# The choice matrix of a further turn moved onto the output buffer, in a one-core encoder layer with 32 experts

## The chip, the cores and the metric

The kernel runs on one core of a Trainium2 chip. The core has five engines, each with an instruction stream of its own: TensorE (matmuls), VectorE, ScalarE, GpSimd and SyncE. They meet through semaphores; 16 DMA engines move data between HBM and SBUF, fed by queues that SyncE (called SP in the profile), ScalarE (ACT) and GpSimd (POOL) issue into. In the profile TensorE is PE, its weight loads are PEld, VectorE is DVE. The metric is the device time of one execution in microseconds, the median of several.

## What is computed

One layer of an encoder, on two requests of 256 tokens each (512 tokens, 1024 values per token, f32): a modulated norm, a projection with spatial gating and pooling, a norm, and then a mixture of 32 experts of which every token takes two. The part that matters here is the last one:

```python
def _hier_moe(h, ...):                       # h: 512 x 1024
    g_sel = argmax(h @ w_router_group)       # one of 4 groups
    top_logit, top_idx = top_k(logits of the 8 experts in the group, 2)
    gate = p_sel * softmax(top_logit)
    ...
    for each expert e, for its tokens xs:
        ys = (silu(xs @ w_exp_gate[e]) * (xs @ w_exp_up[e])) @ w_exp_down[e]
    out[token] += ys * weight
y = LN(alpha * x + gate2 * out)
```

The weights of an expert are two matrices of 1024 x 512 and one of 512 x 1024, f32, 2 MB each.

## The kernel before

The first 450 us or so are the norm, the projection and the mixer; the change doesn't touch them. Behind them runs a loop over the 32 experts, written out in the program of each engine.

**A turn.** An expert works on up to 64 tokens (`CAP`) at a time. TensorE gathers their rows by a matmul with a matrix of zeros and ones (the choice matrix) that VectorE makes by comparing slot numbers, `gate_up` multiplies by `gate_w` and `up_w` (side by side in the two halves of the array), ScalarE takes the silu into `sg_hid`, VectorE multiplies the two halves (`sg_hid<-bank,sg_hid`, L2033), TensorE transposes the product (line 926), ScalarE copies it to `hid_t`, TensorE multiplies by `down_w`, and VectorE evicts the result into `yout`, times a gate that it has written there before (lines 1963, 1965 and 2048). GpSimd stores `yout` to `round_y` in HBM. At the end the rows are gathered from `round_y` and summed.

**Which experts.** Every expert has this main turn. One with more than 64 tokens has further turns, on the same weights with other buffers, all of them with an x in their names: `sel_x` (the choice matrix, 2 KB per partition), `x_rows_x`, `x_t_x` and `hid_t_x` (gathered rows, their transpose, the hidden values) and `yout_x` (the output, 2 KB per partition). In SBUF `x_rows_x`, `x_t_x`, `hid_t_x` and `sel_x` begin at the same place, T0; `yout_x` lies at T0 + 4096. The table `tab` holds for each expert the number of its further turns (`tab[0:1, 0, e]`) and the number of those of all earlier experts (`tab[0:1, 1, e]`). With these inputs there is exactly one further turn in the whole run, that of expert 19; VectorE writes `yout_x` in it (line 2010) once.

**Branches.** For experts 2 to 31 each engine loads the number of further turns and goes either through the plain path or, by a jump to code at the end of its program, through `with_further`, where the main turn and the first further one are interleaved. There TensorE begins with `further_selected`, the gathering matmuls that read `sel_x`.

**What VectorE does for the next expert.** Since a jump is made late, VectorE writes the choice matrix of a possible further turn for every expert from 2 on, whether it has one or not: `further_ahead` (line 1974), ahead of the branch and ahead of the product `sg_hid` of that expert. In the trace this is `sel_x<-next_slots,slot_of`, line 1976, 30 times.

**Waits.** VectorE does its instructions in order, so one that waits holds all behind it. The semaphores of the further turns are `x_sem[...]`: "yo" counts the finished `yout_x` (it starts at 1), "xs" the finished gathering matmuls. `x_st` counts the stores of `yout_x`: it stands at 16 after a small store early in the kernel, and a further turn adds 32, for two stores of 128 KB (lines 570 and 571). Before the change VectorE waits for `x_st` in `further_gate`, before it writes the gate into `yout_x`. TensorE in plain experts does `gate_up`, then a part of the gathering for later experts (`sel_group`), then the transposes of `sg_hid`, the rest of that gathering and the matmuls with `down_w`.

**Weights.** SyncE loads `gate_w` and `up_w` three experts ahead into three buffers, each when the `gate_up` that read the buffer is done (lines 413 and 414), and `down_w` two ahead into two buffers, when the matmuls that read it are done (line 417).

Of the kernel before, what the change touches and what calls it, by code (L numbers as in the profile page):

```python
# [11 lines left out]
TILES = TOK // 128  # L12
# [7 lines left out]
CAP = 64  # L20
ASSIGN = 2 * TOK
FURTHER = ASSIGN // CAP
# [18 lines left out]
def hybrid_encoder(nc, x_prompt, x_sample, c_prompt, c_sample, w_mod, b_mod, w_in, b_in, w_spatial,  # L41
# [3 lines left out]
    bf16, f32, f32r, i32, u32 = mybir.dt.bfloat16, mybir.dt.float32, mybir.dt.float32r, mybir.dt.int32, mybir.dt.uint32  # L45
# [8 lines left out]
    with ctx:  # L54
        base = (nc.sbuf_base + 63) // 64 * 64

        def at(name, shape, dt, off):
            return nc.alloc_sbuf_tensor_at(name, shape, dt, offset=base + off)

        def sem(name):  # L60
            return ctx.enter_context(nc.semaphore(name))
# [69 lines left out]
        tab = at("tab", [1, 2, NEXP + 1], i32, S0 + 2528)  # L131
        slots = at("slots", [128, CAP], f32, S0 + 2816)
        next_slots = at("next_slots", [128, CAP], f32, S0 + 2048)
        T0 = S0 + 9728
# [49 lines left out]
        slot_of = at("slot_of", [128, NEXP, TILES], f32, S0 + 1536)  # L184
        hid_t_x = at("hid_t_x", [128, FC, CAP], f32, T0)
        sg_hid = at("sg_hid", [128, DE], f32, T0 + 36864)
        sel_x = at("sel_x", [128, TILES, 2, CAP], f32r, T0)
        yout = [at(f"yout{i}", [128, 512], f32, o) for i, o in enumerate((T0 + 2048, S0 + 3584, S0 + 5632))]
        x_rows_x = at("x_rows_x", [128, 512], f32, T0)
        x_t_x = at("x_t_x", [128, 2, 4, CAP], f32, T0)  # L190
# [105 lines left out]
        x_st = sem("x_st")  # L296
# [3 lines left out]
        x_sem = {n: sem("x_" + n) for n in ("sl", "xs", "xr", "xtr", "xt", "gum", "silu", "hid", "htr", "ht", "ym", "yo")}  # L300
# [1233 lines left out]
        def _(dve):  # L1534
# [368 lines left out]
            def chosen_pair(out, columns):  # L1903
                return dve.tensor_tensor(out[:, :, :, :],
                                         slots[:, :].rearrange("p (i a s) -> p i a s", i=1, a=1).broadcast_to([128, TILES, 2, CAP]),
                                         columns.rearrange("p a (i s) -> p i a s", s=1).broadcast_to([128, TILES, 2, CAP]), ALU.is_equal)
# [54 lines left out]
            def gate_of_slots(out, first_sem, count, of_first, of_second):  # L1961
                dve.wait_ge(first_sem, count)
                dve.tensor_scalar(out[:, :], gate2_half[1][:, :], of_second, None, ALU.mult).then_inc(first_sem, 1)
                dve.wait_ge(first_sem, count + 1)
                dve.scalar_tensor_tensor(out=out[:, :], in0=gate2_half[0][:, :], scalar=of_first, in1=out[:, :],
                                         op0=ALU.mult, op1=ALU.add).then_inc(first_sem, 1)
                dve.wait_ge(first_sem, count + 2)
# [4 lines left out]
                return more, first  # L1972

            def further_ahead(e):
                dve.wait_ge(dve_selx, 1)
                dve.tensor_tensor(sel_x[:, :, :, :],
                                  next_slots[:, :].rearrange("p (i a s) -> p i a s", i=1, a=1).broadcast_to([128, TILES, 2, CAP]),
                                  slot_of[:, e, :].rearrange("p (i a s) -> p i a s", a=1, s=1).broadcast_to([128, TILES, 2, CAP]),
                                  ALU.is_equal).then_inc(dve_selx, 1)

            def further_counted(e):
                column = slot_of[:, e, :]
                dve.tensor_scalar(column, column, float(CAP), None, ALU.subtract).then_inc(dve_gx, 1)
                dve.tensor_scalar(n0[:, e:e + 1], n0[:, e:e + 1], float(CAP), None, ALU.subtract).then_inc(dve_gx, 1)

            def further_chosen(e, turns):
                further_counted(e)
                column = slot_of[:, e, :]
                dve.wait_ge(x_sem["yo"], turns + 1)
                dve.wait_ge(dve_gx, 6 * turns + 2)  # L1990
                chosen_pair(sel_x, column.rearrange("p (a i) -> p a i", a=1).broadcast_to([128, 2, TILES])).then_inc(x_sem["sl"], 1)

# [4 lines left out]
            def further_gate(e, turns):  # L1997
                dve.tensor_scalar(side[:, 0, 3:4], n0[:, e:e + 1], -0.5, None, ALU.is_gt).then_inc(dve_gx, 1)
                dve.tensor_scalar(side[:, 1, 3:4], n0[:, e:e + 1], -0.5, None, ALU.is_le).then_inc(dve_gx, 1)
                dve.wait_ge(x_sem["yo"], turns + 1)  # L2000
                dve.wait_ge(x_st, 32 * turns + 16)
                gate_of_slots(yout_x, dve_gx, 6 * turns + 4, side[:, 0, 3:4], side[:, 1, 3:4])

            def further_hidden(turns):
# [7 lines left out]
            def further_round(e, turns):  # L2012
                further_chosen(e, turns)
                further_columns(turns)
                further_gate(e, turns)
                further_hidden(turns)
                further_out(turns)
# [32 lines left out]
            def with_further(e):  # L2050
                more, first = turns_of(e)
                dve.wait_ge(dve_g, 2 * (e // 3 + 1) + 2 * e)
                dve.wait_ge(dve_selx, e)
                further_counted(e)
                dve.wait_ge(dve_gx, 6 * first + 2)
                dve.sem_inc(x_sem["sl"], 1)
                further_columns(first)
                hidden(e)
                gate_rows(e)
                further_gate(e, first)  # L2060
                further_hidden(first)
                out_rows(e)
                next_group(e)
                further_out(first)
                with dve.If(more > 1):
                    with dve.Fori(1, more) as r:
                        further_round(e, dve.snap(first + r))

            def expert(e):
# [14 lines left out]
                elif e == 1:  # L2084
                    dve.tensor_scalar(next_slots[:, :], slots[:, :], float(CAP), None, ALU.add).then_inc(dve_selx, 1)
                    hidden(e)
                    dve.wait_ge(m_sem["yo"], e)
                    gate_rows(e)
                    for half, bank in enumerate((B[2], B[4])):
                        dve.wait_ge(m_sem["xtr"], 4 + half)  # L2090
                        columns_in(x_by_expert[:, 2:4, 4 * half:4 * half + 4, :], bank).then_inc(m_sem["xt"], 1)
                    chosen_group(4)
                    out_rows(e)
                else:
                    more = dve.value_load(tab[0:1, 0, bass.ds(e, 1)], min_val=0, max_val=7)
                    dve.wait_ge(m_sem["yo"], e)
                    if e % 3 == 0:
                        sides(e)
                    further_ahead(e)
                    parted(dve, f"dve_{e}", more)  # L2100
                    hidden(e)
                    gate_rows(e)
                    out_rows(e)
                    next_group(e)
                    joined_again(dve, f"dve_{e}")
# [146 lines left out]
```

## Time and profile before

| | us |
|---|---|
| median of 3 runs | 959.89 |
| lowest, highest | 959.08, 962.08 |
| the profiled execution | 962.08 |
| its span, first to last instruction | 960.4 |

The profiled execution is the run with the highest time. TensorE is busy 908.7 us of the span (95%), VectorE 376.8, ScalarE 244.7, GpSimd 113.7. The profile lists groups of instructions with the idle time of their engine just before them and the engine that ended it; "issue" there is a wait that nothing recorded explains. The chain of waits follows the work that ended last back to the start. The granted clock is TensorE's, as a share of 2.4 GHz; it has two levels, 1 and 0.5 (1.2 GHz). The time from a DMA's issue to its landing is listed by tile. Experts are counted from 0 in this text; the 32 evictions of `yout` on VectorE tell in the trace where each ends: expert 18's starts at 733.35 us, expert 19's at 764.26, expert 20's at 782.44.

### The profile page before, as it was taken

The numbers are of one execution on the slowest core, as the hardware profiler recorded it, in microseconds if no ns is written. First come the engines' busy times: TensorE is split into PE (matmuls) and PEld (weight loads), VectorE is DVE, ScalarE is ACT, GpSimd is POOL, SyncE is SP. The second block draws the span as 40 slices with busy tenths as digits, with TensorE's granted clock in tenths as the row PEclk, the third lists the DMA queues.
The fourth block names the chain that finished last, engine by engine and source line by source line (L and its number), as shares of the span: only waits on it lengthen the run. The fifth ranks groups of instructions, "written<-read, shape, count | busy, mean of one in ns | idle before, by whom it ended". The sixth has DMA issues, their size and how long they took to land.

```text
span 960.4 us, 11747 instructions
## 1 busy us (share of the span) xinstructions
PE 908.7 (95%) x4381; PEld 548.4 (57%) x4381; DVE 376.8 (39%) x646; ACT 244.7 (25%) x357; POOL 113.7 (12%) x142
## 2 busy tenths in 40 slices
PE   3999999999999999999999999998997999998994
PEld 2567776888888888786444444444444343443331
DVE  4533443565344236798532232222221221322235
ACT  1432244432233225446411111101101110111024
POOL 2210366000001000000000000000100000000031
PEclk9999999999999999999999999999997999999997
DMA  9985655265565623809999999999999799999974
GB/s 370 347 276 175 257 215 177 90 231 206 202 237 149 180 93 115 274 0 411 388 397 400 419 426 428 426 425 428 427 428 424 307 420 425 426 427 427 422 295 138
DMA packets 47510, 295.53 MB, mean 308 GB/s; under 512 B 5046, under 2 KB 7190, under 8 KB 32082
## 3 DMA queue, kind: packets, MB, share of 16 engines
q1 hardware_dynamic: 37216, 263.99, 68.3%
q0 software_dynamic: 9616, 29.02, 9.0%
q10 hardware_dynamic: 610, 1.66, 0.5%
q8 instruction: 38, 0.62, 0.3%
q14 instruction: 30, 0.25, 0.1%
HBM read 275.81 MB, written 23.09 MB: 311 GB/s over the span
## 4 chain that ended last, share of the span: by engine, by line
PE 89%; DVE 4%; issue 3%; DMA 2%; ACT 2%; POOL 0%; ACTq 0%; POOLq 0%; DVEq 0%
PE bank L624 85%; PE bank L926 2%; DMA cst<-in_consts 1%; DMA y_first<-round_y,pos_y 1%; PE bank L654 1%; DVE st L1558 0%; PE bank L829 0%; PE bank L689 0%; DVE wo_lo L1752 0%; DMA round_y<-yout,store_row 0%; PE bank L908 0%; DVE y_second L2166 0%; DVE y_second L2179 0%; ACT w_hi L1170 0%; POOL y_second L612 0%
## 5 line engine op out<-in xcount | busy, mean ns | idle before, releaser
L624 PE MATMUL bank<-down_w,hid_t 128*64 128x512 f32 x512 | 122.0, 619 | 12.5 <-issue 9.8
L624 PE MATMUL bank<-h_hi,w_hi 128*128 128x512 f32 x320 | 124.8, 390 | 0.3 <-ACT h_hi L1204 0.3
L624 PE MATMUL bank<-h_hi,w_lo 128*128 128x512 f32 x320 | 124.7, 390 | 0.0
L624 PE MATMUL bank<-h_lo,w_hi 128*128 128x512 f32 x320 | 124.5, 397 | 0.0
L624 PE MATMUL bank<-gate_w,x_by_pair 128*64 128x512 f32 x256 | 112.5, 592 | 0.8 <-ACT x_by_pair L1170 0.8
L624 PE MATMUL bank<-up_w,x_by_expert 128*64 128x512 f32 x256 | 112.6, 593 | 0.0
L624 PE MATMUL bank<-gate_w,x_by_expert 128*64 128x512 f32 x256 | 112.6, 593 | 0.0
L624 PE MATMUL bank<-up_w,x_by_pair 128*64 128x512 f32 x256 | 112.5, 592 | 0.0
L1587 DVE TENSOR_TENSOR w_lo<-raw,w_hi 128x1024 fp32r<-128x1024 f32 x56 | 68.5, 1225 | 76.6 <-ACT w_hi L1170 76.5
L1404 ACT ACTIVATE sg_hid<-bank 64x512 f32<-64x512 f32 x33 | 19.5, 592 | 310.2 <-PE bank L624 310.2
L2033 DVE TENSOR_TENSOR sg_hid<-bank,sg_hid 64x512 f32<-64x512 f32 x32 | 22.2, 695 | 176.9 <-ACT sg_hid L1404 176.8
L596 POOL DMA_INDIRECT round_y<-yout,store_row x31 | 31.9, 1028 | 494.8 <-DVE yout L2048 469.4
L624 PEld LDWEIGHTS bank<-down_w,hid_t 128*64 128x64 f32 x512 | 36.9, 141 | 73.5 <-issue 67.4
L624 PEld LDWEIGHTS bank<-gate_w,x_by_pair 128*64 128x64 f32 x256 | 35.0, 137 | 71.2 <-issue 71.2
L624 PEld LDWEIGHTS bank<-gate_w,x_by_expert 128*64 128x64 f32 x256 | 34.8, 137 | 70.3 <-issue 70.1
L2048 DVE TENSOR_TENSOR yout<-bank,yout 128x512 f32<-128x512 f32 x32 | 22.1, 691 | 132.7 <-PE bank L624 128.1
L624 PEld LDWEIGHTS bank<-h_lo,w_hi 128*128 128x128 f32 x320 | 60.1, 188 | 24.3 <-issue 11.7
L1170 ACT ACTIVATE w_hi<-raw 128x1024 fp32r<-128x1024 f32 x56 | 58.9, 1053 | 52.6 <-PE bank L624 51.6
L624 PEld LDWEIGHTS bank<-h_hi,w_lo 128*128 128x128 f32 x320 | 60.1, 188 | 12.8
L624 PEld LDWEIGHTS bank<-h_hi,w_hi 128*128 128x128 f32 x320 | 60.1, 188 | 12.5 <-ACT h_hi L1204 0.7
L624 PE MATMUL bank<-sel_group,h_hi 128*128 128x256 f32 x224 | 61.2, 307 | 0.0
L624 PEld LDWEIGHTS bank<-sel_group,h_hi 128*128 128x128 f32 x224 | 42.4, 189 | 23.6 <-issue 21.9
(329 smaller groups left out, 1313.6 us busy)
## 6 DMA issues: line engine op xcount, KB each, us to landing
down_w<-in_w_exp_down SPq DMA_DIRECT2D x32, 2048.0 KB, 18.0
gate_w<-in_w_exp_gate SPq DMA_DIRECT2D x30, 2048.0 KB, 18.0
up_w<-in_w_exp_up SPq DMA_DIRECT2D x30, 2048.0 KB, 22.7
modraw<-in_w_mod SPq DMA_DIRECT2D x24, 1024.0 KB, 7.1
raw<-in_w_in SPq DMA_DIRECT2D x9, 2048.0 KB, 9.7
round_y<-zrow POOLq DMA_DIRECT2D x6, 2048.0 KB, 7.7
raw<-in_w_branch_b SPq DMA_DIRECT2D x2, 2048.0 KB, 9.4
raw<-in_w_branch_a SPq DMA_DIRECT2D x2, 2048.0 KB, 10.6
```

Of the source, the lines that this page charges most:

```text
L596: pool.indirect_dma_start(round_halves, bass.IndirectOffsetOnAxis(store_row[:, e:e + 1], 0), yout[s][:, :], None, bounds_check=2 * LAST_RO ...
L624: return pe.matmul(out, lhsT, rhs, start=start, stop=stop, skip_group_check=True)
L654: x = pe.transpose(bank[:, 128 * (kc % 4):128 * (kc % 4) + 128], xin[:, i, 128 * kc:128 * kc + 128], ident)
L926: x = pe.transpose(bank[:, CAP * fc:CAP * fc + CAP], view[:, fc, :], ident[CAP:128, CAP:128])
L1170: return act.activation(out, in_, ACT.Copy, scale=scale)
L1404: act.activation(sgb[0:CAP, :], bank[0:CAP, :], ACT.Silu).then_inc(sm["silu"], 1)
L1587: dve.tensor_tensor(w_lo[par][:, :, :], raw[:, u % 2, :, 128 * (b % 4):128 * (b % 4) + 128], w_hi[par][:, :, :].bitcast(f32), ALU.subtract ...
L2033: dve.tensor_tensor(sg_hid[CAP:128, :], B[0][CAP:128, :], sg_hid[0:CAP, :], ALU.mult).then_inc(m_sem["hid"], 1)
L2048: dve.tensor_tensor(yout[s][:, :], B[1][:, :], yout[s][:, :], ALU.mult).then_inc(m_sem["yo"], 1)
```

## The change

`sel_x` moves from T0 to T0 + 4096, where `yout_x` lies. It no longer overlaps `x_rows_x`, `x_t_x` and `hid_t_x`. VectorE then may write `sel_x` only when the `yout_x` of the last further turn has been stored, so `further_ahead` loads the number of earlier further turns and waits for `x_sem["yo"]` and `x_st`; `further_chosen`, which is used for second and later turns, waits for `x_st` too; and `further_gate`, which writes `yout_x`, waits until the gathering matmuls have read `sel_x` instead of waiting for the store.

```diff
-        sel_x = at("sel_x", [128, TILES, 2, CAP], f32r, T0)
+        sel_x = at("sel_x", [128, TILES, 2, CAP], f32r, T0 + 4096)
...
             def further_ahead(e):
+
+                first = dve.value_load(tab[0:1, 1, bass.ds(e, 1)], min_val=0, max_val=FURTHER)
+                dve.wait_ge(x_sem["yo"], first + 1)
+                dve.wait_ge(x_st, 32 * first + 16)
                 dve.wait_ge(dve_selx, 1)
                 dve.tensor_tensor(sel_x[:, :, :, :],
...
                 dve.wait_ge(x_sem["yo"], turns + 1)
+                dve.wait_ge(x_st, 32 * turns + 16)
                 dve.wait_ge(dve_gx, 6 * turns + 2)
...
             def further_gate(e, turns):
...
-                dve.wait_ge(x_sem["yo"], turns + 1)
-                dve.wait_ge(x_st, 32 * turns + 16)
+                dve.wait_ge(x_sem["xs"], turns + 1)
                 gate_of_slots(yout_x, dve_gx, 6 * turns + 4, side[:, 0, 3:4], side[:, 1, 3:4])
```

The instructions of TensorE, ScalarE, GpSimd and SyncE stay as they are. On VectorE two places differ. The first is the start of a plain expert from 2 on: the load of the branch number, `sel_x`, the branch, the product and the gate. The names in brackets are the semaphores waited for: e_yo the evicted `yout` of the expert before, x_yo and x_st those above, e_silu ScalarE's silu. Before:

```order
L2095 TENSOR_LOAD tab
L2095 ISA x2
L1976 TENSOR_TENSOR sel_x<-next_slots,slot_of 128x512 [waits dve_selx,e_yo]
L326 COMPARE_AND_BRANCH
L2033 TENSOR_TENSOR sg_hid<-bank,sg_hid 64x512 [waits e_silu]
```

With the change:

```order
L2099 TENSOR_LOAD tab
L2099 ISA x2
L1976 TENSOR_LOAD tab [waits e_yo]
L1976 ISA x2
L1977 REGISTER_ALU
L1978 ISA [waits x_yo]
L1980 TENSOR_TENSOR sel_x<-next_slots,slot_of 128x512 [waits dve_selx,x_st]
L326 COMPARE_AND_BRANCH
L2037 TENSOR_TENSOR sg_hid<-bank,sg_hid 64x512 [waits e_silu]
```

A second load with its checks, a register operation and two waits have come in between the eviction of the expert before and `sel_x`.

The second place is the gate of a further turn, inside `with_further`. Before:

```order
L1998 TENSOR_SCALAR side<-n_138 128x1 [waits dve_g]
L1999 TENSOR_SCALAR side<-n_138 128x1
L2001 ISA [waits x_yo]
L1962 REGISTER_ALU [waits x_st]
L1963 TENSOR_SCALAR yout_x<-gate_half_142,side 128x512 [waits dve_gx]
```

With the change:

```order
L2003 TENSOR_SCALAR side<-n_138 128x1 [waits dve_g]
L2004 TENSOR_SCALAR side<-n_138 128x1
L1962 REGISTER_ALU [waits x_xs]
L1963 TENSOR_SCALAR yout_x<-gate_half_142,side 128x512 [waits dve_gx]
```

The wait for the store has left this place, and one for the gathering matmuls stands there.

## Rows read from the trace of the kernel before

**Rows 1.** The page's strips, 40 slices of the span, in tenths

```profile
PEclk9999999999999999999999999999997999999997
DMA  9985655265565623809999999999999799999974
```

**Rows 2.** Chain of waits in order of time: start us, us, what

```profile
777.45 0.62 PE bank L926 x4
778.07 12.75 PE bank L624 x64
...
884.96 0.39 ACT hid_t L1170
885.36 0.78 issue
```

**Rows 3.** Tile view of up_w from 776, of down_w from 862: issue and landing

```profile
L414 SPq DMA_DIRECT2D up_w<-in_w_exp_up x1: 425/425/425, 776.4 to 776.4; - x1
...
DMA to landing us min/median/max: 13.4/13.4/13.4
...
L417 SPq DMA_DIRECT2D down_w<-in_w_exp_down x1: 336/336/336, 862.8 to 862.8; - x1
...
DMA to landing us min/median/max: 23.2/23.2/23.2
```

**Rows 4.** Timeline of DVE and POOL: start us, us, what [idle before <-releaser]

```profile
769.01 0.69 DVE L2010 TENSOR_TENSOR yout_x<-bank,yout_x 128x512 f32<-128x512 f32 x1 [2.93 <-PE bank L624]
770.12 0.69 DVE L1976 TENSOR_TENSOR sel_x<-next_slots,slot_of 128x512 fp32r<-128x512 f32 x1 [0.42 <-issue]
...
770.61 0.59 POOL L570 DMA_DIRECT2D round_y<-yout_x  x1 [3.67 <-DVE yout_x L2010]
771.22 0.55 POOL L571 DMA_DIRECT2D round_y<-yout_x  x1
...
776.50 0.69 DVE L2033 TENSOR_TENSOR sg_hid<-bank,sg_hid 64x512 f32<-64x512 f32 x1 [5.69 <-ACT sg_hid L1404]
```

**Rows 5.** Timeline of PE in expert 20

```profile
777.17 0.28 PE L624 MATMUL bank<-sel_group,h_lo 128*128 128x256 f32 x1
777.38 0.69 PE L926 MATMUL bank<-cst,sg_hid 64*128 64x64 f32 x4
```

**Rows 6.** Tile view of yout_x: its two stores, issue to landing

```profile
DMA to landing us min/median/max: 6.7/7.4/8.1
```

**Rows 7.** Timeline of DVE in experts 10, 11 and 31

```profile
613.19 0.69 DVE L2048 TENSOR_TENSOR yout<-bank,yout 128x512 f32<-128x512 f32 x1 [3.95 <-PE bank L624]
613.92 0.69 DVE L1976 TENSOR_TENSOR sel_x<-next_slots,slot_of 128x512 fp32r<-128x512 f32 x1
620.61 0.69 DVE L2033 TENSOR_TENSOR sg_hid<-bank,sg_hid 64x512 f32<-64x512 f32 x1 [6.00 <-ACT sg_hid L1404]
...
925.44 0.69 DVE L2033 TENSOR_TENSOR sg_hid<-bank,sg_hid 64x512 f32<-64x512 f32 x1 [4.28 <-ACT sg_hid L1404]
```

**Rows 8.** PE's timeline behind idle times; one windows row (times, busy, PEclk, DMA, GB/s)

```profile
682.47 3.65 PE L624 MATMUL bank<-down_w,hid_t 128*64 128x512 f32 x16 [1.70 <-issue]
697.47 5.35 PE L624 MATMUL bank<-down_w,hid_t 128*64 128x512 f32 x16 [1.57 <-issue]
727.89 5.35 PE L624 MATMUL bank<-down_w,hid_t 128*64 128x512 f32 x16 [1.85 <-issue]
736.21 0.77 PE L624 MATMUL bank<-h_hi,sel_x 128*128 128x512 f32 x1 [2.97 <-issue]
...
735.50:742.20 6.70, 5.99 (x14) 4.76 (x15) 0.23 (x2) 0.00 (x0) 0.32 (x1) 0.50 1.01 421
...
886.13 5.08 PE L624 MATMUL bank<-down_w,hid_t 128*64 128x512 f32 x16 [1.21 <-ACT hid_t L1170]
900.72 3.65 PE L624 MATMUL bank<-down_w,hid_t 128*64 128x512 f32 x16 [0.47 <-ACT hid_t L1170]
```

**Rows 9.** Timeline of DVE before expert 19

```profile
734.08 0.69 DVE L1976 TENSOR_TENSOR sel_x<-next_slots,slot_of 128x512 fp32r<-128x512 f32 x1
```

## The prediction

> **What bounds the kernel now.** I read the page's strips first, to see where the span goes, then the chain of waits from the only further turn onward, then the timeline of VectorE, GpSimd and TensorE around that turn, and last the places where TensorE stood idle, with the granted clock behind each. In the second half of the span, the expert loop, each slice being 24 us long, the strips show the DMA engines at 9 tenths or more of their time and TensorE's clock at 9, from slice 20 to slice 38, but for one slice at 7 in the clock (720 to 744) and the next at 7 in the DMA engines (744 to 768) [rows 1]. Two limits lie close together. The chain tells which one rules where. After expert 19 it is TensorE back to back: 12.75 us of matmuls from 778.07, with only the four transposes of `sg_hid` (0.62 us) between two such pieces, up to the transposes of expert 28 at 884 [rows 2]. There one piece of 0.78 us called "issue" stands between the copy of `hid_t`, which ends at 884.96 + 0.39 = 885.35, and the first `down_w` matmul at 886.13. The `down_w` load issued at 862.8 landed 23.2 us later, at 886.0 [rows 3], so this piece is a wait for weights, the only one after expert 19 that the chain shows. From 778 to the end, then, what delays TensorE delays the end, less at most 0.78 us.
>
> The change adds a wait for a store only where a further turn came before, so the trace of the turn is what matters. `yout_x` is finished at 769.01 + 0.69 = 769.70, GpSimd issues its two stores at 770.61 and 771.22, VectorE does `sel_x` for expert 20 at 770.12, then stands idle 5.69 us, and does the product `sg_hid` of expert 20 at 776.50 [rows 4]. TensorE reads that product in the transposes at 777.38, right behind its last selection matmul, which starts at 777.17 and lasts 0.28 [rows 5]. So TensorE there has no slack at all to VectorE, while VectorE has 5.69 us before its own product.
>
> **The change part by part.**
>
> *The wait for the store, expert 20.* `sel_x` now lies on `yout_x`, so it can't be written until the store of expert 19's turn has landed. The two stores took 6.7 and 8.1 us from issue to landing [rows 6]. The semaphore needs both; with the longer time on the second store it comes at 771.22 + 8.1 = 779.3, with the longer on the first at 770.61 + 8.1 = 778.7. I take 779.3, since both share one queue and the later one should land later. Behind the waiting `sel_x` on VectorE are queued, in this order, the branch, the product `sg_hid`, the two operations on `yout` and the eviction of `yout`. `sel_x` costs 0.69 and starts some 0.04 after its release, as it does behind `yout` (613.92 against 613.19 + 0.69) [rows 7]. With the same 0.04 before the next operation the product starts at 779.3 + 0.04 + 0.69 + 0.04 = 780.07 and not at 776.50: 3.57 us later, call it 3.55. All of it goes to TensorE, which waits for `sg_hid` with nothing else to do: its six pairs of selection matmuls stand ahead of the transposes and are done by then. GpSimd, ScalarE and the SP queue don't wait on VectorE otherwise; the `gate_w` load for expert 23 hangs on matmuls that come before the stall, the `down_w` load behind it comes as late as TensorE does.
>
> *TensorE's clock after the idle time.* Idle times of TensorE before a matmul, and what followed: 1.70 us, then the 16 `down_w` matmuls in 3.65 us; 1.57 us, then the same in 5.35; 1.85 us, then 5.35; 2.97 us, then 6.7 us at a granted clock of 0.50 (1.2 GHz) in which TensorE was busy 5.99 [rows 8]. A loss is thus nothing, 5.35 - 3.65 = 1.70, or 5.99 / 2 = 3.0. The new idle time of 3.55 is longer than any of these, so the row without a loss is the far end. The nearest is 2.97 us, but that one came only 3 us after another slow stretch, and here TensorE comes from full clock. I take the middle of 1.70 and 3.0: 2.35 us, with 0 and 3.0 kept as ends.
>
> *The weights.* Delayed by 5.9 us, TensorE also frees buffers later. The `up_w` load issued at 776.4 landed 13.4 us later, at 789.8 [rows 3], which is also when the stream comes free for what follows. The next load is the `down_w` one that TensorE releases after expert 20; at a delay of 5.9 it comes just as the stream runs dry, so the stream loses part of the delay but not all of it. Since it lost less, the 0.78 us at 885.36 go: minus 0.78. Ends: 0 (the stream is as late as TensorE) and minus 0.78. In this execution the stretch behind that wait also ran at the lower clock (5.08 us for the matmuls that take 3.65 in expert 29, with an idle time of 0.47 before them instead of 1.21) [rows 8]; 1.43 us more may come back with it. Other executions need not have had that, so it stays in the range only.
>
> *The added load of `first` and its checks, 30 times.* In `further_ahead` a register load, its checks, a register operation and two waits stand before `sel_x`, behind the end of `yout`. The trace doesn't show their time. At 613.19 `yout` starts and at 613.92 `sel_x`, with a branch, one such load and its checks between them: one load costs at most 0.73 us [rows 7]; from below it is 0, as a gain is excluded, nothing being removed there. It lies in VectorE's idle time before the product, which is 6.00 us in most plain experts and 4.28 in the shortest, expert 31 [rows 7]. Cost: 0. Uncovered it would be 30 x 0.73 = 22 us, but each expert would have to lack its 4.28 or more.
>
> *The same load before expert 19.* Here TensorE waits for `sel_x` itself, since `further_selected` is its first work in the further path. `sel_x` ends at 734.08 + 0.69 = 734.77 [rows 9], TensorE starts at 736.21 [rows 8], 1.44 us later, held by its own jump and loads. With 0.73 added 0.71 is left: cost 0.
>
> *The waits in `further_gate`.* Two waits go and one for `x_sem["xs"]` comes. With `x_st` at 16 and `x_sem["yo"]` at 1 from the start, and the selection finished before the transposes that VectorE has already waited for, all three are met: 0. The wait added in `further_chosen` sits in code for a second turn of an expert, which doesn't run: 0.
>
> **The sum:** 3.55 + 2.35 - 0.78 = 5.1 us. The profiled execution has a span of 960.4 and a time of 962.08; the median of the runs is 959.89, 2.2 lower. Most of this difference can be the slow stretches of TensorE, which needn't fall the same way twice. I put the sum on the median: 959.89 + 5.1 = 965.0. On the profiled execution it would be 967.2, or 965.8 if the stretch at 886 goes too.
>
> **The rivals.**
>
> *The store lands before it is needed.* If it lands by 775.7, `sel_x` ends before 776.50 and nothing changes: 959.9. Against it: the 6.7 and 8.1 us, under weight loads that fill the DMA engines; it would have to be 4.5 us or less. The stores share the engines with 2 MB weight loads both before and after the change, so I see no reason for a shorter time.
>
> The Trainium skill ("DMA: Bandwidth & Descriptors", Anatomy of one DMA) puts a GpSimd DMA at about 2.0 us plus its bytes at 436 GB/s; for a store of 128 KB this is an estimate of 2.3 us, and by it the wait would be free. The 6.7 and 8.1 us of the trace speak against that here.
>
> *The weights take the whole delay back.* Not slower, then: 960. If the waits for weights after 778 add up to the delay or more, the DMA stream sets the end and TensorE's stall vanishes in it. For it: the DMA strips at 9, and a load's time to land growing from 13.4 to 23.2 us, as TensorE runs ahead of the stream. Against it: these waits sum to 0.78 us in the chain; it decides only from some 5.9 us on.
>
> *The clock holds.* The stall stays alone: 3.55 - 0.78 = 2.8, 962.7. For it: the idle time of 1.70 us without a loss; against it: the three others.
>
> *It costs more.* A landing 1.5 us later, 3.0 for the clock, nothing back: 3.55 + 1.5 + 3.0 = 8.05, 967.9.
>
> **How the numbers follow.** The forecast, 3.1 to 7 us (963.0 to 966.9): 0.65. The clock holds: 0.12. The store lands early: 0.06. The weights take it back: 0.06. It costs more: 0.11. About 0.3% (2.9 us) is what a measurement of this kernel can tell from no change. Slower: the forecast, the costlier case and a little of the third, 0.78. Same: the rest but 0.02, 0.20. Faster needs slow stretches that happen to vanish: 0.02. The range leaves out the two cases at 960 and the far part of the costly one: 961.9 to 968.0. The likeliest time is 965.0.
>
> **What would show it.** VectorE's `sel_x` of expert 20 starts some 9 us later against the end of `yout_x` and is released by the DMA of `round_y<-yout_x`; the product `sg_hid` follows it without idle time; TensorE shows an idle time of 3 to 4 us before the transposes of expert 20 and there alone; a stretch at clock 0.50 lies behind it; the 0.78 us at expert 28 are gone; in the other plain experts VectorE's idle time before the product is up to 0.7 shorter and the period of 13.37 us (12.75 + 0.62 in the chain) is the same. I am wrong if the stores land in under 5 us, if that period grows, or if expert 19's selection starts more than 0.3 us later behind the `yout` before it.

## The result and the profile after

| | before | with the change |
|---|---|---|
| median, us | 960.38 (959.08 to 962.08, 4 runs) | 967.59 (966.36 to 968.84, 4 runs) |
| ratio to before, 95% interval | | 1.0074 (1.0052 to 1.0096) |
| span of the profiled execution, us | 960.4 | 961.4 |
| its time, us | 962.08 | 963.12 |

The kernel became slower by 7.2 us. A second measurement of the same kernel later gave 965.54 against 961.30, a ratio of 1.0039 (1.0021 to 1.0057). Both measurements together, 17 executions with the profiled ones, have their median at 966.0, against 960.4 of the 106 executions of before in the later measurements. The change costs 4 to 7 us. One execution of all those measured for this text (of the repeated kernel "all but expert 20") took 1335.66 us at a mean granted clock of 0.654 and is left out of the numbers. The profiled execution of the changed kernel, at 963.12 us, is not among the four of the table and lies under every one of them, so its span alone would tell 1 us. That span has to be taken apart.

The strips of the profile after, as [rows 1] of before: TensorE's clock has no slice under 9 in the expert loop, and the DMA strip has one slice of 8 there, where before it had one of 7.

```profile
PEclk9999999999999999999999999999999999999997
DMA  9985655265565523809999999999999899999974
```

VectorE, GpSimd and TensorE around the further turn, from the timeline, as [rows 4] and [rows 5]; in the brackets stands the idle time just before and what ended it:

```profile
767.36 0.69 DVE L2014 TENSOR_TENSOR yout_x<-bank,yout_x 128x512 f32<-128x512 f32 x1 [2.92 <-PE bank L624]
768.96 0.59 POOL L570 DMA_DIRECT2D round_y<-yout_x  x1 [3.67 <-DVE yout_x L2014]
769.57 0.55 POOL L571 DMA_DIRECT2D round_y<-yout_x  x1
774.22 0.59 ACT L1404 ACTIVATE sg_hid<-bank 64x512 f32<-64x512 f32 x1 [10.62 <-PE bank L624]
777.29 0.69 DVE L1980 TENSOR_TENSOR sel_x<-next_slots,slot_of 128x512 fp32r<-128x512 f32 x1 [9.24 <-DMA round_y<-yout_x]
778.01 0.69 DVE L2037 TENSOR_TENSOR sg_hid<-bank,sg_hid 64x512 f32<-64x512 f32 x1
778.85 0.66 PE L926 MATMUL bank<-cst,sg_hid 64*128 64x64 f32 x4 [3.06 <-DVE sg_hid L2037]
```

Before, `sel_x` of expert 20 came 1.11 us after the start of `yout_x` and the product `sg_hid` waited for ScalarE. Now `sel_x` waits 9.24 us for the store, ScalarE's silu has long been done (774.22 + 0.59), the product follows `sel_x` with nothing between, and TensorE stands idle 3.06 us before the transposes. The tile view gives the two stores' time to landing, as [rows 6]:

```profile
DMA to landing us min/median/max: 6.7/7.2/7.7
```

The issue of the second at 769.57 plus 7.7 is 777.27, and `sel_x` starts at 777.29: the later landing is the second store's, as the prediction assumed. Behind the transposes, in the chain of waits (start us, us, what), as [rows 2]:

```profile
769.57 7.70 DMA round_y<-yout_x
...
778.01 0.70 DVE sg_hid L2037
...
778.85 0.66 PE bank L926 x4
779.51 14.44 PE bank L624 x64
793.95 0.62 PE bank L926 x4
794.57 12.75 PE bank L624 x64
```

The piece of 64 matmuls that lasts 12.75 us in the plain experts behind it takes 14.44 here. A row of the view by windows (times, busy us of PE, PEld, DVE, ACT and POOL, then the granted clock, DMA share, GB/s) says why; the clock is 0.51 behind the stall:

```profile
780.80:784.20 3.40, 3.40 (x10) 0.96 (x8) 0.00 (x0) 0.02 (x1) 0.00 (x0) 0.51 1.04 443
```

Then expert 28, where before there was a wait for weights and a slow piece of 5.08 us, as the last rows of [rows 8]:

```profile
888.53 3.65 PE L624 MATMUL bank<-down_w,hid_t 128*64 128x512 f32 x16 [0.47 <-ACT hid_t L1170]
```

To put the two spans side by side I take the starts of the 32 evictions of `yout` on VectorE, and the distances between them. All values are from the two timelines:

```
us                                     before   after    difference
start of the span to yout of expert 19  764.26   762.61   -1.65
yout of expert 19 to that of 20          18.18    22.97   +4.79
20 to 27 (seven plain experts)           93.56    93.56    0.00
27 to 28                                 15.32    13.16   -2.16
28 to the end of the span                69.1     69.1     0.0
sum                                                       +1.0
```

So the change's place costs 4.8 us: 3.1 us of stall (TensorE's transposes start 10.80 us after the end of `yout_x`, before it was 7.68) and 1.7 of clock. Seven plain experts cost nothing, to a hundredth. Expert 28 gives 2.16 back. The 1.65 lie ahead of the `yout` of expert 19, where the change does no more than the added load; 0.42 of them are there when its selection starts (736.21 before, 735.79 after), and the rest falls in the selection and the matmuls behind it, where the granted clock from 735.8 to 745.0 was 0.65 before and 0.81 after.

### The profile page after: what moved, and what is told of

The parts are those of the page before. It is cut to its first block, busy times and chain, and to the rows that moved or that the text cites. A ratio compares the mean times of both kernels' runs of the same rounds, so it can differ in the third digit from the quotient of the medians.

```text
span 961.4 us, 11906 instructions
## 1 busy us (share of the span) xinstructions
PE 906.9 (94%) x4381; PEld 545.6 (57%) x4381; DVE 377.8 (39%) x646; ACT 244.6 (25%) x357; POOL 113.5 (12%) x142
## 4 chain that ended last, share of the span: by engine, by line
PE 86%; DMA 3%; DVE 3%; issue 3%; SPq 2%; ACT 2%; POOL 0%; DVEq 0%; POOLq 0%; ACTq 0%
PE bank L624 83%; PE bank L926 2%; SPq L397 2%; DMA modraw<-in_w_mod 1%; DMA y_first<-round_y,pos_y 1%; DMA round_y<-yout_x 1%; PE bank L829 0%; PE bank L689 0%; DMA round_y<-yout,store_row 0%; DVE wo_lo L1752 0%; PE bank L908 0%; DVE y_second L2170 0%; DVE y_second L2183 0%; DVE sg_hid L2037 0%; ACT w_hi L1170 0%
```

## Experiments

The theory (A) is the prediction's: the wait for the store in expert 20 stalls TensorE through `sg_hid`, and the idle time costs clock behind it. The rivals were that the register load itself costs something (B), that something is lost in each expert (C), and that the place in SBUF matters. Each kernel ran beside the kernel before on the same chip; the ratio is to that.

### Load alone, old place

```diff
             def further_ahead(e):       # in the kernel before
+                first = dve.value_load(tab[0:1, 1, bass.ds(e, 1)], min_val=0, max_val=FURTHER)
+                dve.wait_ge(x_sem["yo"], first + 1)
                 dve.wait_ge(dve_selx, 1)
```

> The kernel before with only the register load of first and the wait for x_sem[yo] added in further_ahead; sel_x stays at T0, no wait for the store. Theory A (the wait for the store in expert 20 and the clock behind it carry the change): within 1 us of the kernel before, VectorE's product sg_hid of expert 20 right behind ScalarE's silu, a period of 13.37 us in plain experts. Rival B (the load itself carries part of it, through the start of expert 19's further path, where TensorE's idle time grew from 2.97 to 4.70 us): 1.5 to 2.5 us slower than before, with an idle time of 4.5 us or more before the first sel_x matmul. Rival C (something in every expert): 5 us or more slower.

Measured: 960.94 against 960.22, ratio 1.0008 (0.9991 to 1.0025). Experts 19 to 20 take 18.17 us, as before. TensorE's idle time before expert 19's first `sel_x` matmul is 3.02, not 4.5 or more. C is out. For B the interval still allows 2.4 us, and the idle time proves less than I had thought (see "Expert 19's start" below); the three loads further down decide more.

### Both waits, old place

```diff
             def further_ahead(e):       # in the kernel before, sel_x still at T0
+                first = dve.value_load(tab[0:1, 1, bass.ds(e, 1)], min_val=0, max_val=FURTHER)
+                dve.wait_ge(x_sem["yo"], first + 1)
+                dve.wait_ge(x_st, 32 * first + 16)
                 dve.wait_ge(dve_selx, 1)
```

> The kernel before with the load and both waits added in further_ahead, sel_x still at T0 and further_gate as before. Theory A: as the changed kernel, 6 to 8 us slower than before, since the wait for the store is there and the place of sel_x is of no weight; VectorE idle some 9 us before sel_x of expert 20. If the place in SBUF mattered instead (rival), it would come out within 2 us of e1_load_only.

Measured: 967.07 against 960.22, ratio 1.0065 (1.0044 to 1.0085). One line more than the kernel above, a wait that no data needs there, brings the whole loss. The place in SBUF is without weight. From its chain of waits:

```profile
769.97 8.55 DMA round_y<-yout_x
...
779.26 0.71 DVE sg_hid L2036
...
780.11 0.71 PE bank L926 x4
780.82 14.09 PE bank L624 x64
```

The store takes 0.85 us longer to land than in the profile of the changed kernel, and the stall is that much longer (TensorE idle 3.91 instead of 3.06).

### The stall filled with matmuls

```diff
                     residual_ahead(e)   # in the changed kernel, TensorE
+                    if e == 20:
+                        for _ in range(3):
+                            mm(B[7][:, :], ident, gate2_half[0][:, :])
                     main_transposes(e)
```

> The changed kernel with three extra 128x512 f32 matmuls (about 0.85 us each) on TensorE in expert 20, before the transposes of sg_hid, into a bank that nobody reads. The stall of 3.06 us stays, but TensorE works through most of it. Theory A with its clock term: 1.7 to 3 us faster than the changed kernel, no stretch at 0.50 behind expert 20's transposes, VectorE's evictions of yout in experts 19 and 20 21.3 us apart instead of 22.97. If the clock has no part in it: as the changed kernel.

Measured: 963.67 against 960.22, ratio 1.0038 (1.0020 to 1.0055): 3.4 us under the kernel with both waits, which ran on the same chip, and 3.45 over before. The chain and a windows row of this kernel:

```profile
768.78 8.15 DMA round_y<-yout_x
...
778.51 0.66 PE bank L926 x4
779.17 12.75 PE bank L624 x64
...
780.00:784.00 4.00, 4.00 (x20) 1.29 (x18) 0.46 (x1) 0.48 (x1) 0.00 (x0) 1.00 1.01 430
```

The transposes still come late, 11.25 us after the end of `yout_x` (10.80 in the changed kernel), but the piece behind them is back at 12.75 us and the clock at 1.00. The loss has two parts, then: a stall that the filling leaves (3.45 us), and a clock loss that it takes away. In the profiles, experts 19 to 20 take 23.53 us with both waits and 21.72 filled. Of these 1.8 us, 0.4 is only a landing that came earlier (transposes 11.25 us after the end of `yout_x` instead of 11.66), and 1.4 is the clock (14.09 + 0.71 against 12.75 + 0.66). By the medians it is 3.4. The means of the same executions differ by 2.9, with a standard error of 0.8, so the 1.4 of the profiles is within what they allow, and the size of the clock's part stays open between 1.4 and 3.4.

### Load moved ahead of the eviction

```diff
                     more = dve.value_load(tab[0:1, 0, bass.ds(e, 1)], min_val=0, max_val=7)
+                    first = dve.value_load(tab[0:1, 1, bass.ds(e, 1)], min_val=0, max_val=FURTHER)
                     dve.wait_ge(m_sem["yo"], e)     # in the changed kernel
...
-                first = dve.value_load(...)         # in further_ahead
```

> The changed kernel with the register load of first moved ahead of the wait for the eviction of yout, beside the load of more, so that it runs while that eviction does. sel_x should start under 0.2 us behind the eviction again, instead of 0.9 to 1.2 us. Theory A: as the changed kernel within 1 us. Rival B: 1.5 to 2 us faster than the changed kernel, TensorE's idle time before the first sel_x matmul of expert 19 back at 3 us.

Measured: 966.94 against 960.22, ratio 1.0055 (1.0035 to 1.0076), as the changed kernel. The edit didn't do what it was meant to. `sel_x` still starts 0.8 to 1.2 us behind the eviction, not under 0.2, so the load's time was not taken out of the path, and this run can't tell whether it would have mattered. TensorE's idle time before expert 19's first `sel_x` matmul is not back at 3 us either:

```profile
728.32 3.65 PE L624 MATMUL bank<-down_w,hid_t 128*64 128x512 f32 x16 [1.05 <-issue]
737.12 0.77 PE L624 MATMUL bank<-h_hi,sel_x 128*128 128x512 f32 x1 [5.14 <-issue]
733.60 0.69 DVE L1978 TENSOR_TENSOR sel_x<-next_slots,slot_of 128x512 fp32r<-128x512 f32 x1 [0.83 <-DVE yout L2050]
```

`sel_x` ends at 734.29, 2.8 us before TensorE starts, so at this place it is not what TensorE waits for. The rows of TensorE show what that idle time hangs on: see "Expert 19's start" below.

### All but expert 20 wait

```diff
+                first = dve.value_load(tab[0:1, 1, bass.ds(e, 1)], min_val=0, max_val=FURTHER)
+                dve.wait_ge(x_sem["yo"], first + 1)
+                if e != 20:                         # in the kernel before
+                    dve.wait_ge(x_st, 32 * first + 16)
```

> As e2_wait_at_old_place (load, both waits, sel_x at T0), but expert 20 alone doesn't wait for the store; the other 29 experts do. Theory A (only the expert right behind the further turn pays): within 1 us of the kernel before. Rival (the waits cost something in every expert, or later ones pay too): 2 us or more above it.

Measured: 962.37 against 960.39, ratio 1.0022 (1.0007 to 1.0038), 2.0 us over and so more than expected; its experts 19 to 20 took 18.18 us, as before. I ran it once more:

> e5_all_but_expert_20 once more, unaltered, because it came out 2.0 us over the kernel before (interval 0.7 to 3.7), where less than 1 was expected. If that was scatter: 0 to 1.5 us over the kernel before. If the loads and the waits that are met at once cost something: 2 us again.

Measured: 960.60 against 960.54, ratio 0.9996 (0.9976 to 1.0015). The 2.0 us did not come again. Taken with the measurements above (4 to 7 us with expert 20's wait), 29 of the 30 waits cost little or nothing, and that of expert 20 makes the loss.

### Three loads

```diff
             def further_ahead(e):       # in the kernel before
+                for _ in range(3):
+                    first = dve.value_load(tab[0:1, 1, bass.ds(e, 1)], min_val=0, max_val=FURTHER)
+                dve.wait_ge(x_sem["yo"], first + 1)
```

> The kernel before with three register loads of first in further_ahead instead of none, then one wait for x_sem[yo]; sel_x at T0, no wait for the store. e1 with one load stood 0.7 us over before, e5 with one load 2.0. If the load costs about 1 us in all, through sel_x coming later in every expert, three cost 3 us or more, sel_x starting some 2 us behind the eviction. If the load is free, as the 4.3 us or more of idle time before the product say: within 1 us of e1.

Measured: 961.50 against 960.54, ratio 1.0008 (0.9988 to 1.0029). Three loads cost no more than one by anything that can be told, and B falls with this as a cause of the loss. The four kernels with loads and no wait in expert 20 lie together, by the means of 47 executions, 0.8 us over their kernels before (standard error 0.4), so up to about 1.5 us for the loads is not excluded. VectorE in a plain expert of this kernel, below it in the changed kernel, and last `sel_x` with the load alone, as [rows 7]:

```profile
612.81 0.69 DVE L2051 TENSOR_TENSOR yout<-bank,yout 128x512 f32<-128x512 f32 x1 [3.94 <-PE bank L624]
615.55 0.69 DVE L1979 TENSOR_TENSOR sel_x<-next_slots,slot_of 128x512 fp32r<-128x512 f32 x1 [2.04 <-issue]
620.23 0.69 DVE L2036 TENSOR_TENSOR sg_hid<-bank,sg_hid 64x512 f32<-64x512 f32 x1 [3.99 <-ACT sg_hid L1404]
```

```profile
612.87 0.69 DVE L2052 TENSOR_TENSOR yout<-bank,yout 128x512 f32<-128x512 f32 x1 [3.94 <-PE bank L624]
614.75 0.69 DVE L1980 TENSOR_TENSOR sel_x<-next_slots,slot_of 128x512 fp32r<-128x512 f32 x1 [1.19 <-issue]
620.29 0.69 DVE L2037 TENSOR_TENSOR sg_hid<-bank,sg_hid 64x512 f32<-64x512 f32 x1 [4.84 <-ACT sg_hid L1404]
```

```profile
614.22 0.69 DVE L1978 TENSOR_TENSOR sel_x<-next_slots,slot_of 128x512 fp32r<-128x512 f32 x1 [0.81 <-DVE yout L2050]
```

`sel_x` comes 2.04, 1.19 and 0.81 us behind the eviction. In the first two the idle time before the product shrinks to 3.99 and 4.84, and the product stays where it was, 7.42 us after the eviction's start in both, as before. A delay under the cover of idle time is free.

### A shorter second store

```diff
-                pool.dma_start(round_y[bass.ds(row, rows), 512:1024], y[64:64 + rows, :]).then_inc(done, 16)
+                pool.dma_start(round_y[bass.ds(row, 1), 512:1024], y[64:65, :]).then_inc(done, 16)
```

> The changed kernel with the second store of a further turn cut from 64 rows to 1 (the second halves of 63 output rows of expert 19's further turn are left out). Theory A: sel_x of expert 20 is released by what is then the later landing, earlier than the 7.7 to 8.6 us of the second store by 0.5 to 2 us; the stall and the time shrink by as much, 0.5 to 2 us under the changed kernel. If the time from issue to landing is fixed and doesn't hang on the bytes: as the changed kernel.

Measured: 966.09 against 960.39, ratio 1.0052 (1.0036 to 1.0068). With 2 KB in place of 128 KB the second store still lands 8.00 us after its issue, the time is that of the changed kernel, and the 0.5 to 2 us expected of a shorter store did not come. From its chain:

```profile
770.14 8.00 DMA round_y<-yout_x
...
779.72 0.66 PE bank L926 x4
780.38 14.38 PE bank L624 x64
```

The first store, of 128 KB and issued 0.6 us earlier into the same queue, landed 6.9 us after its issue here. Whether 2 KB would land sooner with no store ahead of them in the queue was not tried.

### The store issued by ScalarE

```diff
+            def further_store(e, turns):            # ScalarE, in the changed kernel
+                turn = act.snap(e + 1 + turns)
+                act.wait_ge(x_sem["yo"], turns + 2)
+                row = turn * CAP
+                for h in range(2):
+                    act.dma_start(round_y[bass.ds(row, CAP), 512 * h:512 * h + 512], yout_x[64 * h:64 * h + CAP, :]).then_inc(x_st, 16)
...
```

The calls of this function, GpSimd's stores, which are gone, and the small early store that starts `x_st`, which ScalarE issues too, are left out here.

> The changed kernel with the two stores of yout_x (and the small early one that starts x_st) issued by ScalarE's queue instead of GpSimd's; all waits of the change are kept. Theory A: the stall of expert 20 is the time from the end of yout_x to the landing less VectorE's slack of 5.7 us, so it shrinks by what the landing comes earlier. GpSimd needs 0.9 us to issue and the later store lands 7.7 to 8.6 us after that. If ScalarE's stores land within 6 us of the end of yout_x, the stall is gone and the time is that of e5_all_but_expert_20 or of the kernel before (960 to 962.5). If its queue is as slow under the weight loads (8 us or more), it stays at 966 to 967.

Measured: 966.83 against 960.54, ratio 1.0066 (1.0041 to 1.0091). ScalarE issues its first store at 768.78, 0.2 us after the end of `yout_x` where GpSimd took 0.9, and its second at 769.54, 0.9 us after it where GpSimd took 1.5. It wins nothing:

```profile
767.90 0.70 DVE yout_x L2022
...
769.54 9.11 DMA round_y<-yout_x
...
780.24 0.71 PE bank L923 x4
780.95 14.20 PE bank L621 x64
```

The landing takes 9.11 us instead of 7.7 to 8.6. By either queue, and with 128 KB or 2 KB in the second store, the semaphore comes 9.2 to 10.1 us after the end of `yout_x`.

### Fillings in experts 28 and 29

Two extra f32 matmuls in the idle time before `sg_hid` there, in the kernel before and in the changed kernel with the filling of expert 20:

```diff
+                    if e in (28, 29):
+                        mm(B[7][:, :], ident, gate2_half[0][:, :])
+                        mm(B[7][:, 0:256], ident, gate2_half[0][:, 0:256])
                     main_transposes(e)
```

> The kernel before with two extra f32 matmuls (512 and 256 columns, about 1.3 us) on TensorE in experts 28 and 29, in the 1.5 us in which it waits for sg_hid there. They are the two experts without gathering matmuls or residuals at that place. If the slow stretches found behind these waits in some executions (periods of 15.3 and 17.3 us instead of 13.2) come from this idle time: 0.5 to 2 us faster than before. If not: the same, or up to 0.5 us slower.

> The changed kernel with the fillings of e3 and e7 together. Theory A: e7's time plus the bare stall of 3.1 to 4.0 us; under e3 by what e7 gains on the kernel before.

Measured: before with the fillings 960.50 against 960.39, ratio 0.9995 (0.9980 to 1.0010); the changed kernel with all fillings 964.03, ratio 1.0033 (1.0019 to 1.0048). In the profile of the first, expert 28 takes 13.77 us instead of 15.32, but that gain is not in the medians. The second stands 3.5 us over the first: once more the bare stall, 4.0 us in its profile. No version here is faster than the kernel before.

### The changed kernel again

> The changed kernel once more, unaltered, since its median rests on few executions and its one profile (span 961.4) lies under all its timed ones. Theory A: 6 to 7.5 us over the kernel before; in the profile a stall of TensorE of 3.1 to 4.0 us before the transposes of expert 20, a loss of 1.3 to 2.2 us to the clock in the piece of the chain behind it, and an idle time of 4.5 to 5.3 us before expert 19's first sel_x matmul if the down_w matmuls before it ran at full clock, of 3 us if they ran at half. Open: whether the slow stretches that the timed executions have more than those of before (34 us against 24.5) show up at other places too.

Measured: 965.54 against 961.30, ratio 1.0039 (1.0021 to 1.0057), less than the 6 us that I expected. The steps are the expected ones:

```profile
767.91 0.70 DVE yout_x L2014
770.12 8.53 DMA round_y<-yout_x
...
780.24 0.71 PE bank L926 x4
780.95 14.22 PE bank L624 x64
```

A table of the distances between evictions from all profiles ties it together (ordinary arithmetic on the timelines; with the early load the piece behind the stall took 14.92 us, the longest of all):

```
us                          19 to 20   27 to 28
before                      18.18      15.32
load alone                  18.17      17.28
three loads                 18.17      15.36
all but 20                  18.18      15.28
all but 20, again           18.18      16.54
changed                     22.97      13.16
changed, again              23.64      14.87
both waits, old place       23.53      14.85
short second store          23.23      14.86
store by ScalarE            23.63      14.86
early load                  24.41      14.86
filled 20                   21.72      13.34
filled 20, 28, 29           22.15      13.16
before, filled 28, 29       18.17      13.77
```

The last line but one confirms the clock's part. With a stall as long as with both waits at the old place (transposes 11.68 us after the end of `yout_x`, there 11.66), the one filled in 20, 28 and 29 takes 22.15 us instead of 23.53: again 1.4 us of clock.

## Why the prediction held, step by step

**What bounds the kernel.** Right. Where TensorE is the chain, its delay goes to the end: the seven experts behind the stall take 93.55 to 93.57 us in every profile, before and after.

**The wait for the store, 3.55 us forecast.** Right in mechanism and size. The transposes start 10.80 to 11.71 us after the end of `yout_x` in the kernels with the wait, 7.68 without: a stall of 3.1 to 4.0. The medians of the filled kernels give 3.45 and 3.5 us for the bare stall. That the later landing is the second store's, which the forecast took without a row for it, came true: 7.7 us in the changed kernel, 8.1 in [rows 6].

**The clock, 2.35 us forecast, ends 0 and 3.0.** Right in mechanism, the size open. In the chain the piece behind the stall lost 1.3 to 2.2 us in the six profiles with the wait and no filling (14.09 to 14.92 us against 12.75), so the size in the profiles is nearer 1.7, the first of the two rows that I took the middle of, than 3.0. The medians and means of the filling give 2.9 to 3.4, within their scatter. The mean granted clock of the timed executions points the same way. Twice its distance from 1, times the span, is an estimate of the time at the lower level: on average 24.5 to 26.7 us in the kernel before, 31 to 35 in the kernels with both waits, the early load, the short second store, ScalarE's store and the first measurement of the changed one, and 25.3 with the filling. A stretch that loses 1.7 us lasts 3.4, so one or two of them behind expert 20 make up 3.4 to 6.8 of the 7 to 10.5 us more. Where the rest lies in the timed executions is not shown: in the second measurement of the changed kernel it was 27.6 us in all, against 26.7 of its kernel before, and that one was 2 us faster than the first. The difference between the two measurements, 7.2 and 4.2 us, is thus of the size of the scatter in slow stretches.

**The weights, minus 0.78, and up to 1.43 more.** The wait for the `down_w` load went, as forecast; what came back in all did not follow the term. In all profiles without expert 20's wait for the store but one expert 28 takes 15.28 us or more (the exception is the filled one, 13.77); in those with it and no filling, 13.16 to 14.87. The idle time before its `down_w` matmuls fell from 1.21 to 0.47 us in all six profiles with the wait and no filling, 0.74 less. In one of them the slow stretch went too, and 2.16 us came back. In the other five it stayed and took 0.3 us more than before, 5.35 us for matmuls that took 5.08, so that only 0.46 came back (15.32 to 14.86). From the changed kernel, measured again:

```profile
889.75 5.35 PE L624 MATMUL bank<-down_w,hid_t 128*64 128x512 f32 x16 [0.47 <-ACT hid_t L1170]
```

**The load, 0 forecast, at most 0.73 us each.** The cost was right, the bound wrong. I read the bound from two starts, 613.19 and 613.92, between which the load ran under the eviction. Where it stands behind the wait for the eviction it takes 0.8 to 1.2 us, and a further one adds 0.62 ((2.04 - 0.81) / 2). VectorE's idle time before the product so became 0.9 to 1.2 us shorter in plain experts, not up to 0.7 as the signs said. Nothing hung on that, since 3.99 us of idle time were left with three.

**Expert 19's start, 0 forecast.** In the changed kernel's two profiles the cost was right, but I had named a test for it, the selection starting more than 0.3 us later behind the `yout` before it, and by that test I should have been wrong. The two rows of the changed kernel that answer to the third and fourth of [rows 8]:

```profile
727.44 3.65 PE L624 MATMUL bank<-down_w,hid_t 128*64 128x512 f32 x16 [0.16 <-issue]
735.79 0.47 PE L624 MATMUL bank<-h_hi,sel_x 128*128 128x512 f32 x1 [4.70 <-issue]
```

Against the eviction the selection comes 1.7 us later (735.79 - 731.20 = 4.59, before 2.86), and the idle time has grown from 2.97 to 4.70. Against the start of the `down_w` matmuls it comes at the same time: 8.35 us, before 8.32. The `down_w` matmuls before it ran at full clock here and at half in [rows 8], 3.65 us and 5.35. With the load alone it is 5.35 us of matmuls and 3.02 idle, 8.37 in all; with the early load 3.65 and 5.14, 8.80. In 12 of the 14 profiles the distance is 8.3 to 8.9 us and `sel_x` ends 0.4 to 2.9 us before the selection starts. So what holds the selection there began before the matmuls ended. That it is the fetch of the code of the further path I only suppose. The test should have been set against the start of TensorE's last work. The cost was not 0 everywhere, though. With three loads, and with ScalarE's stores, the selection starts 0.14 us behind the end of `sel_x`, 9.05 and 8.75 us after the start of the `down_w` matmuls: there VectorE holds it, and the loads cost up to 0.7 and 0.4 us against the 8.32 of before.

**The rivals.** *The store lands early*: it would have had to come within 6.0 us of the end of `yout_x`; it took 9.2 to 10.1 in eight profiles. The estimate of 2.3 us by the Trainium skill ("DMA: Bandwidth & Descriptors", Anatomy of one DMA) does not hold beside these weight loads: GpSimd's two stores of 128 KB took 6.7 to 8.7 us from issue to landing, and the one of 2 KB 8.0. *The weights take it back*: their wait gave back 0.74 us and no more. *The clock holds*: in no profile without the filling. *It costs more*: the first measurement (967.59) lay near this rival's 967.9, the second (965.54) near the forecast of 965.0.

**The number.** 965.0 was forecast, 5.1 us over before. The first measurement is 2.6 us over it, the 17 executions together 1.0. In the six profiles with the wait and no filling, the two places of the table add 4.6 to 5.8 us to the 33.50 of before in five, and 2.6 in the first. That the five lie so near 5.1 is in part luck: the stall was up to 0.5 us longer than its term, the clock's loss mostly smaller than 2.35, and less than 0.78 came back at expert 28. The kernel before is no fixed mark either, since the unfilled kernels without expert 20's wait took 15.28 to 17.28 us for experts 27 to 28.

## What to carry to other kernels

Moving a tile onto another one's memory exchanges one hazard for another: ask who reads the new neighbour last. Here it was a compute engine before and a store to HBM after, and beside this full stream of loads the store ended 9.2 to 10.1 us after its data were ready. A wait in an in-order engine must be priced at the work queued behind it: `sel_x` itself was not needed by anyone, since expert 20 has no further turn, but the product behind it was. And the stall of 3.1 to 4.0 us on TensorE cost a third to a half as much again in clock in the profiles (1.3 to 2.2 us); independent matmuls in the gap brought that part back.

## What I had not expected of the hardware

Neither a shorter second store nor another queue made the landing earlier: 8.00 us for 2 KB behind a store of 128 KB, 7.7 to 8.6 for 128 KB from GpSimd, 9.11 from ScalarE's queue, all with the DMA engines at a share of 0.99 to 1.05 from 769 to 778 us.

The distance from the start of TensorE's last `down_w` matmuls to its first work in the jumped-to path was 8.3 to 8.5 us where these matmuls took 5.35 us or more, and 8.35 to 8.9 where they took 3.65 (`sel_x` not holding it), so a slow stretch of 1.7 us just ahead of the jump cost nothing.

The same kernel scattered by 8 us on one chip (957.24 to 965.30 in 31 executions of the kernel before), with the granted clock of single executions between 0.982 and 0.993; one profile of a change of 0.7% can show a seventh of it, as the first one here did.
